# Causal mask as a tenth bfloat16 matmul, scatters issued without waiting, attention's fillers rearranged

## The reference

```python
def mla(h, cos, sin, ...):                    # layer 0: 8 heads, 128 + 64 (rotary) dims of q and k, 128 of v
    for i in range(S // Q_BLOCK):             # four blocks of 128 queries
        q0, q1 = i * Q_BLOCK, (i + 1) * Q_BLOCK
        s = (jnp.einsum('bqhd,bkhd->bhqk', q_nope[:, q0:q1], k_nope[:, :q1])
             + jnp.einsum('bqhr,bkr->bhqk', q_rope[:, q0:q1], k_rope[:, :q1]))
        mask = jnp.arange(q0, q1)[:, None] >= jnp.arange(q1)[None, :]
        s = jnp.where(mask, s.astype(jnp.float32), -jnp.inf)
        p = jax.nn.softmax(s, axis=-1).astype(v.dtype)
        outs.append(jnp.einsum('bhqk,bkhd->bqhd', p, v[:, :q1]))
    ...
    return o @ w_o

def moe_swiglu(h, router, w_gate, w_up, w_down):   # layer 1: the two best of 8 experts for each token
    logits = (xf @ router).astype(jnp.float32)
    top_v, top_i = lax.top_k(logits, TOP_K)
    ...                                            # tokens sorted by expert, in blocks
    yb = lax.map(expert_block, (xb, block_e)).reshape(P, D)
    y = jnp.zeros((N, D), h.dtype).at[buf_tok].add(yb * buf_gate[:, None].astype(yb.dtype))
```

## Time and profile before

| | |
|---|---|
| time, median of 3 runs | 1029.93 us (1028.6 to 1030.96) |
| time of the profiled execution | 1028.6 us |
| its span | 1027.1 us |
| granted TensorE clock, mean | 0.998 of full speed |
| attention, first score matmul to the last head's output | 79.5 to 183.1 us of the span |
| routing and scatter | about 593 to 647 us |
| expert jobs | from about 605 us on |

### The profile page before, as it was taken

One profiled execution on the slowest core, in us unless ns is written; L12 is line 12 of the kernel. 1 busy time (PEld: TensorE's weight loads), 2 busy tenths in 40 slices (PEclk: granted clock), 3 DMA queues, 4 the chain that ended last, 5 costly groups with the idle time before them and its releaser, 6 DMA issues.

```text
span 1027.1 us, 15232 instructions
## 1 busy us (share of the span) xinstructions
PE 1012.5 (99%) x5570; PEld 871.4 (85%) x5570; DVE 596.8 (58%) x840; ACT 451.4 (44%) x602; POOL 70.4 (7%) x135
## 2 busy tenths in 40 slices
PE   8999999999999999999999999999999999999997
PEld 7878887788888888888888999999987888888883
DVE  6677777254344444343436760100689889888986
ACT  6445555244141322222124410010667777777764
POOL 2200000000000001010000011000000000000050
PEclk9999999999999999999999999999999999999999
DMA  9021422535463627273614749896999999999996
GB/s 293 2 82 43 136 69 76 150 104 162 140 182 101 203 81 217 93 214 97 211 35 152 274 154 338 268 341 191 338 370 386 365 393 368 388 369 392 368 395 223
DMA packets 150013, 225.00 MB, mean 219 GB/s; under 512 B 16916, under 2 KB 97812, under 8 KB 149968
## 3 DMA queue, kind: packets, MB, share of 16 engines
q1 hardware_dynamic: 138464, 187.98, 54.6%
q0 software_dynamic: 10688, 35.87, 10.1%
q10 hardware_dynamic: 816, 0.54, 0.2%
HBM read 196.40 MB, written 29.02 MB: 219 GB/s over the span
## 4 chain that ended last, share of the span: by engine, by line
PE 86%; DVE 6%; DMA 3%; ACT 2%; issue 1%; SPq 1%; POOLq 0%; ACTq 0%; DVEq 0%
PE bank L1229 22%; PE bank L1231 22%; PE bank L1230 22%; PE bank L1655 8%; PE bank L1679 4%; PE bank L1411 1%; DMA u_raw<-in_moe_w_down 1%; DMA h<-in_x 1%; PE bank L1241 1%; DVE w_lo L1850 1%; PE bank L1402 1%; DMA u_raw<-in_moe_w_up 1%; PE bank L1631 1%; PE bank L1550 1%; PE bank L1581 1%
## 5 line engine op out<-in xcount | busy, mean ns | idle before, releaser
L2334 DVE TENSOR_TENSOR u_lo<-u_raw,u_hi 128x2048 fp32r<-128x2048 f32 (+1 forms) x104 | 209.4, 2047 | 13.2 <-ACT u_hi L1075 12.7
L1075 ACT CAST u_hi<-u_raw 128x2048 fp32r<-128x2048 f32 (+1 forms) x104 | 178.3, 1723 | 62.3 <-DMA u_raw<-in_moe_w_up 39.6
L1229 PE MATMUL bank<-big_hi,w_lo 128*128 128x512 f32 (+1 forms) x368 | 136.5, 371 | 0.0
L1230 PE MATMUL bank<-big_lo,w_hi 128*128 128x512 f32 (+1 forms) x368 | 136.4, 371 | 0.0
L1231 PE MATMUL bank<-big_hi,w_hi 128*128 128x512 f32 (+1 forms) x368 | 136.4, 371 | 0.0
L1850 DVE TENSOR_TENSOR w_lo<-stage_own,w_hi 128x1024 fp32r<-128x1024 f32 (+1 forms) x89 | 103.4, 1207 | 11.9 <-ACT w_hi L823 11.8
L1012 ACT ACTIVATE scratch<-bank 128x512 f32<-128x512 f32 x21 | 12.5, 597 | 216.3 <-PE bank L1231 216.3
L1229 PE MATMUL bank<-u_hi,nx_lo 128*128 128x512 f32 (+1 forms) x288 | 106.5, 370 | 0.0
L1231 PE MATMUL bank<-u_hi,nx_hi 128*128 128x512 f32 (+1 forms) x288 | 104.5, 363 | 0.0
L1230 PE MATMUL bank<-u_lo,nx_hi 128*128 128x512 f32 (+1 forms) x288 | 104.4, 363 | 0.0
L2118 DVE TENSOR_TENSOR scratch<-scratch,bank 128x512 f32<-128x512 f32 x21 | 14.4, 687 | 150.8 <-ACT scratch L1012 150.8
(11 more groups left out here) (343 smaller groups left out, 1734.6 us busy)
## 6 DMA issues: line engine op xcount, KB each, us to landing
u_raw<-in_moe_w_gate SPq DMA_DIRECT2D x68, 512.0 KB, 8.8
u_raw<-in_moe_w_up SPq DMA_DIRECT2D x68, 512.0 KB, 10.7
u_raw<-in_moe_w_down SPq DMA_DIRECT2D x64, 512.0 KB, 7.7
stage_own<-in_ffn_w_gate SPq DMA_DIRECT2D x21, 512.0 KB, 5.6
stage_own<-in_ffn_w_up SPq DMA_DIRECT2D x21, 512.0 KB, 9.2
stage_own<-in_ffn_w_down SPq DMA_DIRECT2D x21, 512.0 KB, 4.7
xbuf<-scratch POOLq DMA_DIRECT2D x21, 496.0 KB, 6.5
u_raw<-in_moe_w_down SPq DMA_DIRECT2D x8, 1024.0 KB, 8.6
```

The source lines that it names most:

```text
L1075: s.copy(u_hi[u % HIS][0:rows, 0:size], u_raw[u % RAWS][0:rows, 0:size]).then_inc(n_hi, 1)
L1229: t_.matmul(dst, st_lo, mv_hi, start=start, stop=False, skip_group_check=check)
L1230: t_.matmul(dst, st_hi, mv_lo, start=False, stop=False, skip_group_check=check)
L2334: v.tensor_tensor(u_lo[u % RAWS][0:rows, 0:size], u_raw[u % RAWS][0:rows, 0:size], u_hi[u % HIS][0:rows, 0:size], ALU.subtract).then_inc(n ...
```

## The change

Five edits. (1) The mask is added by PE: a sixth matmul in each block's group, with an identity matrix in bfloat16 as weights and the mask, now in bfloat16, as the moving 128 columns, accumulates into the block's own columns; DVE's addition and its wait for itself go. (2) POOL builds the second identity before it signals `consts_ready`. (3) The seven waits between the eight scatters go; the wait for all eight stays. (4) `q2_out(0, 1)` on ACT, the copy of the second head's rotary queries out of bank 4, moves behind the third exponential of the first head. (5) The eight `wo` units are placed differently, on ACT and DVE alike.

```diff
-        causal = sb("causal", [P, P])
+        ident_b = sb("ident_b", [P, P], BF16)
+        causal = sb("causal", [P, P], BF16)
@@ POOL, start
-            link(g.memset(ident[:, :], 0.0))
-            g.affine_select(out=ident[:, :], in_=ident[:, :], compare_op=ALU.not_equal, fill=1.0, base=0,
-                            pattern=[[-1, P]], channel_multiplier=1).then_inc(consts_ready, 1)
+            g.memset(ident[:, :], 0.0)
+            link(g.memset(ident_b[:, :], 0.0))
+            for m in (ident, ident_b):
+                last = g.affine_select(out=m[:, :], in_=m[:, :], compare_op=ALU.not_equal, fill=1.0, base=0,
+                                       pattern=[[-1, P]], channel_multiplier=1)
+            last.then_inc(consts_ready, 1)
@@ POOL, scatter
             for c in range(2 * T):
-                if c:
-                    pool.wait_ge(scattered, 16 * c)
                 pool.indirect_dma_start(out=xbuf, out_offset=bass.IndirectOffsetOnAxis(ap=dest[:, c:c + 1], axis=0),
                                         in_=xn[:, c % T, :], in_offset=None).then_inc(scattered, 16)
             pool.wait_ge(scattered, 16 * 2 * T)
@@ ACT, exps(hd)
-                        if pair == 0 and hd == 0 and qb == T - 2:
+                        if pair == 0 and hd == 0 and qb == T - 1:
                             q2_out(0, 1)
@@ ACT and DVE
-            attention(H // 2 - 2, True, lambda place: [split("wo", k) for k in ((0,), (1,), (2, 3), (4,))[place]])
+            attention(H // 2 - 2, True, lambda place: [split("wo", k) for k in ((0,), (1, 2), (3,), (4, 5))[place]])
-            attention(H // 2 - 1, False, lambda place: [split("wo", k) for k in ((5,), (6, 7), (), ())[place]])
+            attention(H // 2 - 1, False, lambda place: [split("wo", k) for k in ((6,), (7,), (), ())[place]])
@@ PE, scores(hd)
-                        t_.matmul(dst[:, 0:n], q2[:, hd, tok(qb)], kr_lo[:, 0:n], start=False, stop=False)
-                        t_.matmul(dst[:, 0:n], q2[:, hd, tok(qb)], kr_hi[:, 0:n], start=False, stop=True
+                        for kr in (kr_lo, kr_hi):
+                            t_.matmul(dst[:, 0:n], q2[:, hd, tok(qb)], kr[:, 0:n], start=False, stop=False)
+                        t_.matmul(dst[:, tok(qb)], ident_b[:, :], causal[:, :], start=False, stop=True
                                   ).then_inc(scores_done, 1)
@@ DVE, largest(qb)
                         dve.wait_ge(scores_done, pair * 8 + col + 1)
-                        own = bank[qb][:, qb * P:(qb + 1) * P]
-                        link(v.tensor_tensor(own, own, causal[:, :], ALU.add))
                         v.tensor_reduce(neg_max[:, col:col + 1], bank[qb][:, 0:(qb + 1) * P], AX.X, ALU.max, negate=True
                                         ).then_inc(max_ready, 1)
```

## The result

| | before | after |
|---|---|---|
| median of 4 runs | 1030.07 us (1028.6 to 1030.96) | 1037.47 us (1036.23 to 1038.67) |
| ratio, 95% interval | | 1.0074 [1.0055, 1.0092] |
| profiled execution, its span | 1028.6, 1027.1 | 1036.58, 1034.6 |
| granted clock of the span | 0.998 | 0.995 |

The kernel became slower by 0.74%. I had said +1.7 us and a range up to 1035.0, so the result lies outside it. Some 2.0 of the 7.5 us of span are the attention's, where I had forecast 1.7. The other 5.5 arise behind the scatters, an edit that I had priced at nothing.

What follows compares the result with a forecast made beforehand. PE, busy 99% of the span, was taken as the bound, with at most 1.6 us to win in attention. Six heads' masks +2.26 and two heads -0.58 gave +1.7 us: 1030.3 profiled, 1031.6 against the median, range 1029.0 to 1035.0.

Steps and rivals of the forecast that it cites:

- Scatter: Eight scatter issues before the experts, waits removed: gain 0, cost 0 unless expert weights come late, with 13.9 us of slack.
- rival C: Scatter burst of 4.2 MB starves the expert weights: no wait by either estimate; about 1038 or 1039 if doubled; chance 0.04.
- My own sign for it: Sign of being wrong: PE's time outside attention changes by more than 0.5 us.
- Without waits they take 8 us: The eight scatter issues, each 0.96 us long, stretch over 37 us with waits and would take 8 without.
- Mask, 0.376 a head: Mask matmuls on PE: blocks 1 to 3 cost 0.107 each, block 0 0.055; 3.0 us for eight heads.
- anything but 0.1: Sign of being wrong: a mask matmul shifts the next group on PE by anything but 0.1 us.
- rival B: Type changes around the 32 mask matmuls: 0.82 or 1.26 a head, 1035 or 1038; decides from 0.44; chance 0.21.
- The two heads that give back, -0.58: Third pair's second and last pair's first head: earlier hand-over and shorter softmax put PE 0.58 us earlier, both masks included.
- Start, 0: Two more short POOL rows before PE's dummy matmuls at the kernel's start: cost 0, bounds 0 and 0.5 us.
- q2_out, 0: ACT's copy out of bank 4, moved behind the first head's third exponential: cost 0, bounds 0 and 0.3 us.
- The extra split behind the previous softmax costs nothing: Place 1 of wo: softmax ends 1.0 earlier, a split takes 1.15, DVE's next row at most 0.2 later, no wait.
- Sum: Whole kernel: +2.26 - 0.58 = +1.7 us, 1030.3 on the profiled execution, 1031.6 against the median.

Runs made afterwards that it cites:

- e2: Kernel before with only the seven waits between the eight scatters removed: ratio 1.0050.
- e1: Kernel after with the seven waits between the eight scatters put back, the other changes kept: ratio 1.0022.
- e5: Kernel after, unwaited scatters kept, with PE's expert loop written out as straight code without the jump: ratio 1.0075.
- e9: Kernel after, unwaited scatters kept, with PE raising its expert counter once per pair of columns, by 2: ratio 1.0078.
- e4: Kernel after with its eight unwaited scatters begun only when PE has done the fifth unit of the expert phase: ratio 1.0035.
- e12: Kernel after with its scatter waits back and the mask's matmul issued twice in each of the 32 groups: ratio 1.0047 against the kernel before.
- e6: Kernel before with the mask on PE in all heads and its weights built; scatter waits, q2_out and wo places as before: ratio 1.0021.
- e8: Kernel before with the mask on PE only in the last pair's first head, plus the new places of the wo splits: ratio 0.9990.
- e16: Kernel after with seven scatters in a burst and the eighth behind a wait for all seven: ratio 1.0019.
- e17: Kernel after, all eight scatters in flight, with a long-met wait in front of each of the last seven: ratio 1.0022.

## Why the prediction was wrong, step by step

**Where it failed: "Scatter. ... PE does not wait for these rows before or after. So the gain is 0. The cost is 0 unless expert weights come late".** The weights did not come late, and rival C, which I had for this burst, was priced for the weights too. What came in place of it is a stop of PE without a releaser and a late row of ACT: 5.1 to 5.4 us by e2 and e1, 3.8 to 6.4 in single profiles (e5 3.8, e2 3.9, after 5.4, e9 6.4), where the two highest are those with a lower clock behind the stop. Removing the waits from before (e2) brought it, restoring them in after (e1) took it away: that is shown. Why it happens is not. Excluded by runs are the mask, the jump into the loop, the number of PE's counts and plain write bandwidth; with the reservations above also GpSimd's queue with plain transfers and bytes in flight. What is left is an unbroken row of eight indirect scatters in GpSimd's own stream. One sign points there: in all five profiles with a stop (after, e2, e4, e5, e9) the last stop ends 1.4 to 1.6 behind the end of the eighth issue, and ACT's late row starts 0.1 to 0.2 behind that, so both seem held by one thing that ends with the row of issues. What it is stays open; GpSimd's descriptors, the delivery of semaphore counts and the profiler's own recording, which every run on record carried, were not separated. My own sign for it, PE's time outside attention changing by more than 0.5, came out at 5.4. "Without waits they take 8 us" was short too: from the first start to the end of the last they took 9.9, since 0.3 lies between two issues.

**Mask, 0.376 a head: 0.05 too small, and spread otherwise.** Measured 0.43 on average. In the first head the four groups became 0.05, 0.07, 0.13 and 0.14 longer; I had 0.055, 0.107, 0.107, 0.107, and by my own sign ("anything but 0.1") the price by group was wrong. The rows show where the rest lies: the matmul behind a mask starts soon, not 0.11 later, and the one after that is late.

```profile
81.65 0.23 PE L1395 MATMUL bank<-causal,ident_b 128*128 128x128 bf16 x1
81.69 0.47 PE L1231 MATMUL bank<-kn_hi,qn_lo 128*128 128x512 f32 x1
82.00 0.39 PE L1232 MATMUL bank<-kn_lo,qn_hi 128*128 128x512 f32 x1
```

Here 0.31 lies between two matmuls of 512 columns that stand 0.23 apart elsewhere. Six heads cost 2.6 instead of 2.26. The measured 0.43 to 0.44 lies at rival B's deciding point, 0.44, and the 0.22% of e1 just beyond the 0.2% that I had set there; its 0.82 and 1.26 are far off. e12 shows that a second mask costs no more than its columns.

**The two heads that give back, -0.58: measured -0.55.** Most parts came out. In the last pair, after:

```profile
157.99 0.69 DVE L2054 TENSOR_TENSOR big_lo<-bank,big_hi 128x512 fp32r<-128x512 f32 x1
...
161.53 0.62 DVE L2027 TENSOR_REDUCE neg_max<-bank 128x1 f32<-128x128 f32 x2
...
165.45 0.49 DVE L2036 TENSOR_SCALAR scratch<-scratch,row_inv 128x512 f32<-128x512 f32 x1
```
```profile
165.99 0.66 PE L1405 MATMUL bank<-ident,scratch 128*128 128x128 f32 x4 [0.25 <-DVE scratch L2036]
```

At the start of these two heads' scores PE stands 2.06 later than before (144.20 after, 142.14 before), and at the matmul behind the turn 1.51 (166.40 and 164.89): -0.55. Less the 2.06, DVE's row for the low part is 0.69 earlier (0.72 forecast), the maxima begin 0.46 later (0.45), and the softmax lasts 4.41 instead of 5.41, the 1.0 that I took. The wait for the low part is gone and one wait is left, 0.25 listed where I had said about 0.5. But the same net comes out with the old places of wo (e6): what the earlier hand-over gives, the later softmax takes.

**Start, 0: measured -0.09** (79.42 against 79.51). **q2_out, 0: right.** The copy ends at 84.06 + 0.58 = 84.64, and PE uses the bank at 84.87:

```profile
84.06 0.58 ACT L911 CAST q<-bank 128x512 fp32r<-128x512 f32 x1
```

**"The extra split behind the previous softmax costs nothing"**: true in the kernel after, whose masks cover it, and wrong without them: 0.4 in e8.

**Sum.** Forecast +2.26 - 0.58 = +1.7; the rows give +1.98 up to the experts, and e1 measures 1.0022, 2.3 us. That alone would have been 1032.3, in the range and 0.7 above the 1031.6 forecast. The scatters' 5 us put the time outside. I had given 0.04 to any harm from that edit, because my price counted only what PE's program waits for.

## What to carry to other kernels

Moving a cheap operation from a half-idle engine to the full one pays only where the full one waits: of eight heads one did, and the mask there alone is the fastest version. Before taking waits out of a row of transfers that nobody waits for, measure, or leave one in: eight unbroken scatters cost 5 us on an engine that they have nothing to do with, and there was nothing to gain. One real wait ahead of the eighth was enough here (e16), and so were long met waits in all seven gaps (e17); one met wait alone was not tried. When fillers are moved, check the due time of every part behind the moved one.

## What the hardware showed that I had not expected

- PE can stop for "issue", 0.4 or 1.0 us at a time between single matmuls, while GpSimd issues eight indirect scatters in an unbroken row; ACT's row that needs PE's count comes about 6.6 us late (617.69 for about 611), at the moment at which PE's last stop ends. With a real wait ahead of the last one or two, or met waits in all seven gaps, neither was seen; with four in flight that row came 0.9 to 1.2 late and PE didn't stop. Begun 12 us later (e4), the same eight cost 1.0035 against 1.0022, with one stop of 0.4.
- DMA engines at 401 GB/s of plain writes from SyncE's queue stopped none of the same matmuls; the scatters' rate was 385.
- Behind 3 us of stops the granted clock went to 0.50, 1.2 GHz, in two profiles (after, e9) and stayed at 1.00 in two others (e2, e5): 5.4 and 6.4 us lost in all against 3.9 and 3.8.
- A bfloat16 matmul of 128 columns among float32r ones costs 0.11 on average (0.43 / 4); in front of 384 and 512 columns 0.08 of it shows on the second matmul behind it.
